# Expert weights of a mixture-of-experts layer loaded in two halves of the model dimension

## Chip, cores and metric

The kernel runs on one core of one Trainium2 chip. The metric is device time in microseconds (us) of one launch; lower is better. The time of the kernel before is the median of 3 runs.

## What is computed

One trunk layer (DEPTH = 1) over 384 tokens of width 1024 in f32: a parallel token mixer, then a fine-grained mixture of experts, then a norm. The part around the change is the mixture of experts:

```
h = rmsnorm(x) * (1 + scale) + shift
scores = sigmoid(h @ w_router)                  # 64 experts in 8 groups
combine = top-8 of the best 4 groups, normalised, x 2.5
hid = silu(h @ we_g[e]) * (h @ we_u[e])          # for each expert e: 1024 -> 256
routed = sum over e of (hid * combine[:, e]) @ we_d[e]      # 256 -> 1024
shared = (silu(h @ ws_g) * (h @ ws_u)) @ ws_d
out = routed + shared
```

The weights of one expert are gate 1024x256, up 1024x256 and down 256x1024, 1 MiB (1.049 MB) each in f32; all 64 experts have to come in from HBM once. With 384 tokens and 8 choices each, an expert has 48 tokens on average.

## The kernel before

The mixer comes first, then the router, then the experts. Experts are worked two at a time, as 32 pairs (`PAIRS`), p = 0 to 31. A pair gives each expert 64 slots (`SLOTS`) for its tokens; experts that have more tokens are finished afterwards by three "duo" rounds (`DUOS`), p = 32 to 34, which take 32 slots a time, with the weights loaded again for those experts (`load_item`), and by a loop over what is left.

For a pair p TensorE does: `gate_up(p)` (L1029, 16 matmuls that fill one bank: the loop runs over 8 chunks k of the model dimension and over the 2 experts n), `tokens_of(p + 1)` (L976, L979, the transposes of the next pair's gathered tokens), `slots_of(p + 2)` (L931), `hidden_T(p)` (L1041), `scatter(p - 1)` (L1063, the outputs of the pair before added to the tokens' rows), and `down(p)` (L1056, 8 matmuls). An f32 matmul stands as two in the trace, so gate_up shows 32 and down 16. VectorE and ScalarE turn the results of each step into the next one's input. GpSimd gathers the token rows of a pair with an indirect DMA (L520): 128 rows of 1088 f32 values, 4352 bytes; slots without a token are dropped by the bounds check.

The weights lie in `ring`, four places of one expert each. Pair p has slot s = p % 2, that is places 2s and 2s + 1, so a pair's weights overwrite those of pair p - 2. All weight loads are issued by SyncE (SP) on one DMA queue, in program order; each DMA is spread over the 16 DMA engines. Weights of pair p are loaded when its slot is free: gate and up after `gate_up(p - 2)` has counted the semaphore `gate_up_done`, and down after `down(p - 2)` has counted `down_done`. In the load of gate and up (L411, L412) each of the 128 partitions gets one contiguous piece of 8192 bytes: `w_eg` and `w_eu` are viewed so that partition i holds rows 8i to 8i + 7 of the matrix one after the other, and chunk k of the matmul takes row 8i + k of each partition. TensorE waits for all four loads of its pair by `gate_up_slot{s}`, 16 counts for each DMA:

```
sp.wait_ge(sem("gate_up_done"), p - 1)
for n in range(2):
    load_gate_up(sp, (2 * p + n) * P, 2 * s + n, f"gate_up_slot{s}")
sp.wait_ge(sem("down_done"), 2 * (p - 1))
for n in range(2):
    load_down(sp, (2 * p + n) * P, 2 * s + n, f"down_slot{s}")
```

Pairs 0 and 1 are loaded by `first_expert`, earlier, as soon as the mixer's weights have left the ring. Pairs 2 to 31 are loaded by the loop above.

Of the kernel before, what the change touches and what calls it, by code (L numbers as in the profile page):

```python
# [12 lines left out]
P = 128  # L13
D = 1024
KC = D // P
# [13 lines left out]
PAIRS = E // 2  # L29
# [11 lines left out]
CELL = 2048  # L41
# [3 lines left out]
EXPERT = 3 * CELL  # L45
# [135 lines left out]
def trunk_kernel(nc, A, outs, consts, dists):  # L181
    y_prompt, y_sample, new_f, new_b = outs
    ctx = ExitStack()
    with ctx:
        def sb(name, shape, dt=F32):
            return ctx.enter_context(nc.sbuf_tensor(name, shape, dt))

        ring = sb("ring", [P, NSLOT * EXPERT])
# [30 lines left out]
        def sem(name):  # L219
            if name not in sems:  # L220
                sems[name] = ctx.enter_context(nc.semaphore(name))
            return sems[name]
# [137 lines left out]
        w_eg = A["w_exp_gate"].rearrange("o e (p k) f -> (o e p) (k f)", p=P)  # L360
        w_eu = A["w_exp_up"].rearrange("o e (p k) f -> (o e p) (k f)", p=P)
# [45 lines left out]
        def load_gate_up(sp, row, e, landed):  # L407

            w = ring[:, e * EXPERT:(e + 1) * EXPERT]
            src = (lambda a: a[row:row + P, :]) if isinstance(row, int) else (lambda a: a[bass.ds(row, P), :])  # L410
            sp.dma_start(w[:, 0:CELL], src(w_eg)).then_inc(sem(landed), 16)  # L411
            sp.dma_start(w[:, CELL:2 * CELL], src(w_eu)).then_inc(sem(landed), 16)  # L412

        def load_down(sp, row, e, landed):

            w = ring[:, e * EXPERT:(e + 1) * EXPERT]
            src = w_ed[row:row + P, :] if isinstance(row, int) else w_ed[bass.ds(row, P), :]
            sp.dma_start(w[:, 2 * CELL:3 * CELL], src).then_inc(sem(landed), 16)
# [7 lines left out]
        def _(sp):  # L426
# [5 lines left out]
            for name in PIECES:  # L432
# [5 lines left out]
                landed = sem(f"piece_slot{PLACE[name]}")  # L438
# [36 lines left out]
            def load_item(n, e_slot, load, landed, count):  # L475
                there = sp.value_load(column(tab_valid, n), min_val=0, max_val=1)
                with sp.If(there > 0):
                    e = sp.value_load(column(tab_expert, n), min_val=0, max_val=E - 1)
                    load(sp, e * P, e_slot, landed)
                with sp.Else():  # L480
                    sp.sem_inc(sem(landed), count)

            for p in range(2, LAST + 1):
                s = p % 2
                if p == PAIRS:
                    sp.wait_ge(sem("table_ready"), 1)
                sp.wait_ge(sem("gate_up_done"), p - 1)
                for n in range(2):
                    if p < PAIRS:
                        load_gate_up(sp, (2 * p + n) * P, 2 * s + n, f"gate_up_slot{s}")  # L490
                    else:
                        load_item(2 * (p - PAIRS) + n, 2 * s + n, load_gate_up, f"gate_up_slot{s}", 32)
                sp.wait_ge(sem("down_done"), 2 * (p - 1))
                for n in range(2):
                    if p < PAIRS:
                        load_down(sp, (2 * p + n) * P, 2 * s + n, f"down_slot{s}")
                    else:
                        load_item(2 * (p - PAIRS) + n, 2 * s + n, load_down, f"down_slot{s}", 16)
# [109 lines left out]
        def _(pe):  # L608
# [70 lines left out]
            for k in range(KC):  # L679
                pe.wait_ge(sem("scaled_A" if k % 2 else "scaled_V"), k // 2 + 1)  # L680
                ins = mm(o[:, :], hT_scaled[:, k, 0:P], win0.rearrange("p (k n) -> p k n", k=KC)[:, k, :], start=(k == 0), stop=(k == KC - 1))
# [8 lines left out]
            for k in range(KC):  # L690
                q = k % 4 * 32
                ins = mm(o[q:q + 32, :], shift_rep[:, k, :], win0.rearrange("p (k n) -> p k n", k=KC)[:, k, :], start=(k < 4), stop=(k >= KC - 4))
# [7 lines left out]
            for g in range(4):  # L700
                ins = nc.tensor.transpose(o[:, g * P:(g + 1) * P], shift_row[:, g * P:(g + 1) * P], ident)
# [37 lines left out]
            for t in range(TT):  # L739
                for name, nat in (("q", q_nat), ("k", k_nat)):  # L740
# [5 lines left out]
                    for h in range(H):  # L746
                        ins = nc.tensor.transpose(o[:, h * P:(h + 1) * P], nat[:, t, h * P:(h + 1) * P], ident)
# [3 lines left out]
            for d in range(2):  # L751
                pe.wait_ge(sem("kw_ready"), d + 1)
                o = bank(f"state{d}")
                for h in range(H):
                    ins = mm(o[:, h * P:(h + 1) * P], kw[:, d, h * P:(h + 1) * P], v_nat[:, 0, h * P:(h + 1) * P], start=True, stop=True)
# [5 lines left out]
            for h in range(H):  # L761
                ins = mm(o[:, h * P:(h + 1) * P], kT[:, h, 0:P], qT[:, h, 0:P], start=True, stop=True)
            done(ins)
            for h in range(H):
                o = bank(f"sc_lat{h}")
                for j in range(2):
                    ins = mm(o[:, j * LAT:(j + 1) * LAT], kT[:, h, (1 + j) * P:(2 + j) * P], qT[:, h, CTX:T], start=True, stop=True)
# [4 lines left out]
            for h in range(H):  # L772
                ins = mm(o[:, h * P:(h + 1) * P], sc_sb[:, 4, h * P:(h + 1) * P], v_nat[:, 0, h * P:(h + 1) * P], start=True, stop=True)
            done(ins)
            pe.wait_ge(sem("state_in"), 32)
            for t in (1, 2):
                o = bank(f"o{t}")
                for h in range(H):
                    emptied(pe, f"sc_lat{h}")
                    for j in range(2):  # L780
                        ins = mm(o[:, h * P:(h + 1) * P], sc_sb[:, h, j * LAT + (t - 1) * P:j * LAT + t * P],
                                 v_nat[:, 1 + j, h * P:(h + 1) * P], start=(j == 0), stop=(j == 1))
                done(ins)
                for d, name in ((0, "cross_f"), (1, "cross_b")):
                    o = bank(f"{name}{t}")
                    for h in range(H):
                        ins = mm(o[:, h * P:(h + 1) * P], qT[:, h, t * P:(t + 1) * P], S0[:, d, h, :], start=True, stop=True)
# [17 lines left out]
            for m in range(KC):  # L805
# [6 lines left out]
                if m == 5:  # L812
                    for t in range(TT):
                        pe.wait_ge(sem("ret_ready"), t + 1)
                        o = bank(f"retT{t}")
                        for h in range(H):
                            ins = nc.tensor.transpose(o[:, h * P:(h + 1) * P], g_nat[:, t, h * P:(h + 1) * P], ident)
# [122 lines left out]
            for t in range(TT):  # L940
                for u in range(t + 1):
                    ins = mm(o[:, t * E:(t + 1) * E], cbf[:, 0 if u == t else 1, :], sel_bf[:, u, :], start=(u == 0), stop=(u == t))
            done(ins)
            o = bank("count")
            for t in range(TT):
                ins = mm(o[0:E, 0:1], sel_bf[:, t, :], cbf[:, 1, 0:1], start=(t == 0), stop=(t == TT - 1))
# [5 lines left out]
            for t in range(TT):  # L952
                ins = nc.tensor.transpose(o[0:E, t * P:(t + 1) * P], r_rank[:, t, :], ident)
# [44 lines left out]
            landed = LAST // 2 + 1  # L998
# [20 lines left out]
            def gate_up(p):  # L1019
                s = p % 2  # L1020
                if p:
                    pe.wait_ge(sem("xT_ready"), 2 * p)
                    pe.wait_ge(sem("hid_ready"), p)
                else:
                    last_in(0)
                pe.wait_ge(sem(f"gate_up_slot{s}"), 64 * (p // 2 + 1))
                for k in range(KC):
                    for n in range(2):
                        ins = mm(ps[0][n * SLOTS:(n + 1) * SLOTS, :], xT[:, k, n * SLOTS:(n + 1) * SLOTS], expert(2 * s + n)[0][:, k, :, :],  # L1029
                                 start=(k == 0), stop=(k == KC - 1))  # L1030
                ins.then_inc(sem("gate_up_done"), 1)

            def hidden_T(p):
# [104 lines left out]
            for p in range(LAST):  # L1138
                if p < PAIRS:
                    gate_up(p)  # L1140
                else:
                    pe.wait_ge(sem("xT_ready"), 2 * p)
                    pe.wait_ge(sem("hid_ready"), p)
                    pe.wait_ge(sem(f"gate_up_slot{p % 2}"), 64 * (p // 2 + 1))
                    gate_up_duo(p % 2)
                tokens_of(p + 1)
                if p + 2 < PAIRS:
                    slots_of(p + 2)
                elif p + 2 <= LAST:
                    slots_of_duo(p + 2)  # L1150
                hidden_T(p)
                if p:
                    scatter(p - 1)
                if p < PAIRS:
                    down(p)
                else:
                    pe.wait_ge(sem("hidT_ready"), p + 1)
                    pe.wait_ge(sem(f"down_slot{p % 2}"), 32 * (p // 2 + 1))
                    pe.wait_ge(sem("rest_ready"), 2 * p)
                    down_duo(p % 2)  # L1160
            scatter(LAST - 1)

            def further(q):
                p = q + LAST
                pe.wait_ge(sem("gate_up_slot1"), q * 64 + 64 * landed)
                pe.wait_ge(sem("xT_ready"), p * 2)
                pe.wait_ge(sem("hid_ready"), p)
                stand_alone(pe, "pe_passed")
                gate_up_duo(1)
                slots_next(q)  # L1170
                hidden_T(p)
                pe.wait_ge(sem("hidT_ready"), p + 1)
                pe.wait_ge(sem("rest_ready"), p * 2)
                pe.wait_ge(sem("down_slot1"), q * 32 + 32 * landed)
                stand_alone(pe, "pe_passed")
                down_duo(1)
                pe.wait_ge(sem("lo_ready"), p * 2 + 2)
                pe.wait_ge(sem("summed"), p * 6)
                stand_alone(pe, "pe_passed")
                for g in range(6):  # L1180
                    if g == 2:
                        pe.wait_ge(sem("expert_ready"), q + (DUOS + 2))
                    if g >= 4:
                        pe.wait_ge(sem("summed"), p * 6 + (g - 3))
                    scatter_duo_tile((slotT[:, 0, :], slotT_half[:, DUOS, :]), g)
                tokens_next(q)
# [872 lines left out]
```

## Time and profile before

| what | value |
|---|---|
| runs | 1014.66, 1017.45, 1017.86 us; median 1017.45 |
| the profiled execution | 1013.35 us, span 1011.4 us |
| granted TensorE clock, mean | 0.992 of full speed |
| busy: PE, DVE, ACT, POOL | 95%, 52%, 22%, 5% of the span |
| DMA traffic | 301.57 MB, mean 298 GB/s over the span |
| pairs 0 to 31 on TensorE | about 435 us to 950 us of the span |

The page shows one profiled execution, in us from the start of its span. Its own time is 1.95 us longer than its span, and 4.1 us below the median of the runs. PE is TensorE's matmuls, PEld its weight loads, DVE is VectorE, ACT is ScalarE, POOL is GpSimd, SP is SyncE; a "q" behind a name is the engine's queue of issues. The DMA share is the time that packets took, summed and divided by 16 engines; packets in flight on one engine overlap a little, so a full stretch reads slightly over 1. In the rows on DMA queues q1 holds what SyncE issues (the weights) and q0 what GpSimd issues (the gathers); packets of 4 bytes are the counts on a semaphore at the end of a DMA.

### The profile page before, as it was taken

Reading aid. Unit: us, or ns where it says so; the run is one execution under the profiler, and the core shown is the slowest. Engines: PE = TensorE matmul, PEld = TensorE weight load, DVE = VectorE, ACT = ScalarE, POOL = GpSimd, SP = SyncE. Lnnn points to the kernel's source line nnn. Section 1 sums busy time; section 2 is a strip of 40 time slices with the busy share of each in tenths; the row PEclk is TensorE's granted clock in tenths of the full one; section 3 lists DMA queues with packets and bytes.
Section 4 is the critical chain, followed back from the end, with each engine's and each line's share of the span. In section 5 each row is a group of like instructions: output and inputs, shape, how many; then the busy total and the mean of one; then the engine's idle time right before and its main releaser. Section 6 shows DMA issues by size and latency. Waiting matters only on the chain. (4 is left out here: it accounts for less than half of the span.)

```text
span 1011.4 us, 11592 instructions
## 1 busy us (share of the span) xinstructions
PE 961.5 (95%) x4287; PEld 449.4 (44%) x4322; DVE 524.6 (52%) x1089; ACT 221.2 (22%) x423; POOL 55.0 (5%) x71
## 2 busy tenths in 40 slices
PE   4999999999999999899999999999999999999891
PEld 2346445755655547634334343433434343343440
DVE  2202510885695944635454554545455454545666
ACT  4202102010000034222222222222222222222222
POOL 1010000100000000010000000000000000000000
PEclk9999999999999999999999999999999999999997
DMA  9992223207465469059999999999999999999921
GB/s 334 391 336 85 84 83 119 80 2 286 171 226 179 156 249 396 35 230 420 421 421 418 420 420 418 421 419 417 416 421 416 418 406 420 414 417 410 374 112 64
DMA packets 66587, 301.57 MB, mean 298 GB/s; under 512 B 6992, under 2 KB 7176, under 8 KB 39392
## 3 DMA queue, kind: packets, MB, share of 16 engines
q1 hardware_dynamic: 59376, 281.19, 69.5%
q0 software_dynamic: 7152, 19.60, 5.1%
q8 instruction: 36, 0.59, 0.2%
q14 instruction: 23, 0.19, 0.1%
HBM read 303.54 MB, written 3.80 MB: 304 GB/s over the span
## 5 line engine op out<-in xcount | busy, mean ns | idle before, releaser
L1029 PE MATMUL bank<-ring,QK 128*64 128x512 f32 x1024 | 225.2, 592 | 0.0
L1029 PEld LDWEIGHTS bank<-ring,QK 128*64 128x64 f32 x1024 | 73.5, 137 | 146.4 <-issue 146.4
L1912 DVE TENSOR_TENSOR hT<-bank,hT 128x512 f32<-128x512 f32 x210 | 129.2, 683 | 3.4 <-PE bank L1107 2.3
L1063 PE MATMUL bank<-Fm,VG 128*128 128x512 bf16 x544 | 123.2, 379 | 5.3 <-DVE S L1943 3.3
L1056 PE MATMUL bank<-ring,VG 128*64 128x512 f32 x512 | 116.9, 598 | 0.5 <-ACT VG L1388 0.5
L666 PE MATMUL bank<-ring,hT 128*128 128x512 f32 x240 | 103.8, 593 | 0.0
L1903 DVE SCALAR_TENSOR_TENSOR VG<-VG,cw,bank 128x256 f32<-128x256 f32 x32 | 15.4, 480 | 143.3 <-issue 136.9
L1921 DVE TENSOR_TENSOR Fm<-bank,Fm 128x512 f32<-128x512 f32 x64 | 44.3, 692 | 85.1 <-ACT Fm L1395 82.9
L673 PE MATMUL bank<-hT,ring 128*128 128x384 f32 x256 | 85.4, 487 | 0.0
L1063 PEld LDWEIGHTS bank<-Fm,VG 128*128 128x128 bf16 x576 | 56.3, 98 | 65.1 <-DVE S L1943 4.8
L1395 ACT CAST Fm<-bank 128x512 bf16<-128x512 f32 x64 | 37.5, 586 | 208.2 <-PE bank L1056 208.2
L666 PEld LDWEIGHTS bank<-ring,hT 128*128 128x128 f32 x240 | 45.4, 190 | 56.9 <-issue 56.3
L1056 PEld LDWEIGHTS bank<-ring,VG 128*64 128x64 f32 x512 | 33.9, 136 | 68.6 <-issue 68.0
L673 PEld LDWEIGHTS bank<-hT,ring 128*128 128x128 f32 x256 | 48.3, 190 | 34.5 <-issue 1.7
L1377 ACT ACTIVATE VG<-bank 128x256 f32<-128x256 f32 x35 | 13.4, 384 | 167.4 <-PE bank L1029 163.1
L1927 DVE TENSOR_TENSOR Fm<-Fm 128x512 bf16<-128x512 f32 x64 | 43.9, 686 | 2.8
L673 PE MATMUL bank<-Fm,ring 128*128 128x384 f32 x128 | 42.6, 486 | 0.0
L845 PE MATMUL bank<-ring,U 128*128 128x512 f32 x96 | 42.1, 594 | 0.0
L1398 ACT CAST Fm<-Fm 128x512 bf16<-128x512 f32 x64 | 39.7, 620 | 7.7 <-DVE Fm L1921 7.7
L1382 ACT COPY QK<-bank 128x512 f32<-128x512 f32 x70 | 37.6, 589 | 7.9 <-PE bank L976 7.9
L1297 ACT ACTIVATE S<-bank 128x384 f32<-128x384 f32 x16 | 7.8, 491 | 124.5 <-PE bank L673 124.5
L1459 DVE SCALAR_TENSOR_TENSOR AB<-ring,condr,AB 128x512 f32<-128x512 f32 x42 | 31.6, 752 | 1.5
(356 smaller groups left out, 889.6 us busy)
## 6 DMA issues: line engine op xcount, KB each, us to landing
ring<-in_w_exp_gate SPq DMA_DIRECT2D x69, 1024.0 KB
ring<-in_w_exp_up SPq DMA_DIRECT2D x69, 1024.0 KB
ring<-in_w_exp_down SPq DMA_DIRECT2D x69, 1024.0 KB
ring<-in_w_ada SPq DMA_DIRECT2D x12, 2048.0 KB, 10.3
ring<-in_w_in SPq DMA_DIRECT2D x10, 2048.0 KB, 16.9
ring<-in_w_four_out SPq DMA_DIRECT2D x2, 2048.0 KB, 8.1
ring<-in_w_out SPq DMA_DIRECT2D x2, 2048.0 KB, 11.1
ring<-in_w_ret_out SPq DMA_DIRECT2D x1, 2048.0 KB, 14.1
```

The source lines that it names most:

```text
L666: ins = mm(o[:, :], h[:, k, t * P:(t + 1) * P], w[:, k, :], start=(k == 0), stop=(k == KC - 1))
L673: ins = mm(o[:, 0:T], w[:, k, m * P:(m + 1) * P], rhs[:, k, :], start=(k == 0), stop=(k == kc - 1))
L845: ins = mm(o[:, :], mergedT[:, k, t * P:(t + 1) * P], w[:, k, :], start=(k == 0), stop=(k == KC - 1))
L1029: ins = mm(ps[0][n * SLOTS:(n + 1) * SLOTS, :], xT[:, k, n * SLOTS:(n + 1) * SLOTS], expert(2 * s + n)[0][:, k, :, :], start=(k == 0), sto ...
L1056: ins = mm(ps[2 + h][n * SLOTS:(n + 1) * SLOTS, :], hidT[:, j, n * SLOTS:(n + 1) * SLOTS], expert(2 * s + n)[1][:, j, h * 512:(h + 1) * 51 ...
L1063: ins = mm(ps[banks[g]][:, :], slotT[:, k, t * P:(t + 1) * P], y[:, h * 512:(h + 1) * 512], start=(n == 0), stop=(n == 2))
L1382: nc.scalar.copy(halves[n], ps[4 + n][:, :].rearrange("p (k s) -> p k s", k=4)).then_inc(sem("xT_ready"), 1)
L1395: nc.scalar.copy(y_hi[:, h * 512:(h + 1) * 512], ps[2 + h][:, :]).then_inc(sem("hi_ready"), 1)
L1398: nc.scalar.copy(y_mid[:, h * 512:(h + 1) * 512], y_rest[:, h * 512:(h + 1) * 512]).then_inc(sem("mid_ready"), 1)
L1912: v.tensor_tensor(into, o, into, ALU.add).then_inc(sem("summed"), 1)
L1921: v.tensor_tensor(y_rest[:, cut], ps[2 + h][:, :], y_hi[:, cut], ALU.subtract).then_inc(sem("rest_ready"), 1)
L1927: v.tensor_tensor(y_lo[:, cut], y_rest[:, cut], y_mid[:, cut], ALU.subtract).then_inc(sem("lo_ready"), 1)
```

## The change

The gate and up loads of pairs 2 to 31 are each cut in two along the model dimension. A half is 4 of the 8 rows that a partition holds: 4096 of its 8192 bytes. TensorE counts a new semaphore, `gate_up_half_done`, behind the matmuls of chunk k = 3, the last that reads the first half; SyncE then issues the four first halves (gate and up of two experts) of pair p when `gate_up(p - 2)` is half through, and the four second halves when it is through. TensorE still waits for both halves before `gate_up(p)`: the count it waits for is 128 a pair where it was 64. Loads of pairs 0 and 1, of the duo rounds, and all down loads are as they were.

```diff
+        def load_gate_up_half(sp, row, e, half, landed):
+
+            cut = slice(half * CELL // 2, (half + 1) * CELL // 2)
+            w = ring[:, e * EXPERT:(e + 1) * EXPERT]
+            sp.dma_start(w[:, 0:CELL][:, cut], w_eg[row:row + P, cut]).then_inc(sem(landed), 16)
+            sp.dma_start(w[:, CELL:2 * CELL][:, cut], w_eu[row:row + P, cut]).then_inc(sem(landed), 16)
+
...
                 if p == PAIRS:
                     sp.wait_ge(sem("table_ready"), 1)
+                if p < PAIRS:
+                    sp.wait_ge(sem("gate_up_half_done"), p - 1)
+                    for n in range(2):
+                        load_gate_up_half(sp, (2 * p + n) * P, 2 * s + n, 0, f"gate_up_slot{s}")
                 sp.wait_ge(sem("gate_up_done"), p - 1)
                 for n in range(2):
                     if p < PAIRS:
-                        load_gate_up(sp, (2 * p + n) * P, 2 * s + n, f"gate_up_slot{s}")
+                        load_gate_up_half(sp, (2 * p + n) * P, 2 * s + n, 1, f"gate_up_slot{s}")
...
-                pe.wait_ge(sem(f"gate_up_slot{s}"), 64 * (p // 2 + 1))
+                pe.wait_ge(sem(f"gate_up_slot{s}"), 64 + 128 * (p // 2))
                 for k in range(KC):
                     for n in range(2):
                         ins = mm(ps[0][n * SLOTS:(n + 1) * SLOTS, :], xT[:, k, n * SLOTS:(n + 1) * SLOTS], expert(2 * s + n)[0][:, k, :, :],
                                  start=(k == 0), stop=(k == KC - 1))
+                    if k == KC // 2 - 1:
+                        ins.then_inc(sem("gate_up_half_done"), 1)
                 ins.then_inc(sem("gate_up_done"), 1)
```

The counts that the duo rounds and the last loop wait for are raised to match.

On SyncE's queue, the place where the loads of pair 2 begin (`ring` is the weights' buffer, the names behind `in_` are the inputs), before the change:

```order
L411 DMA ring<-in_w_exp_gate 128x2048 [waits gate_up_done]
L412 DMA ring<-in_w_exp_up 128x2048
L411 DMA ring<-in_w_exp_gate 128x2048
L412 DMA ring<-in_w_exp_up 128x2048
L418 DMA ring<-in_w_exp_down 128x2048 [waits down_done]
L418 DMA ring<-in_w_exp_down 128x2048
```

Each later pair up to 31 repeats these six. The same place with the change:

```order
L418 DMA ring<-in_w_exp_gate 128x1024 [waits gate_up_half_done]
L419 DMA ring<-in_w_exp_up 128x1024
L418 DMA ring<-in_w_exp_gate 128x1024
L419 DMA ring<-in_w_exp_up 128x1024
L418 DMA ring<-in_w_exp_gate 128x1024 [waits gate_up_done]
L419 DMA ring<-in_w_exp_up 128x1024
L418 DMA ring<-in_w_exp_gate 128x1024
L419 DMA ring<-in_w_exp_up 128x1024
L425 DMA ring<-in_w_exp_down 128x2048 [waits down_done]
L425 DMA ring<-in_w_exp_down 128x2048
```

Ten DMAs stand where six stood, and the first four of them wait for TensorE's middle mark; no load has moved past a load of another matrix or pair. On TensorE no instruction moves.

## Rows read from the trace of the kernel before

**Rows 1.** The page: span, engine busy in 40 slices, DMA share and rate.

```profile
PE 961.5 (95%) x4287; PEld 449.4 (44%) x4322; DVE 524.6 (52%) x1089; ACT 221.2 (22%) x423; POOL 55.0 (5%) x71
...
PE   4999999999999999899999999999999999999891
...
DMA  9992223207465469059999999999999999999921
```

**Rows 2.** TensorE's timeline: start, length (us), line, output and inputs, count.

```profile
465.01 7.04 PE L1029 MATMUL bank<-ring,QK 128*64 128x512 f32 x32
...
481.09 7.04 PE L1029 MATMUL bank<-ring,QK 128*64 128x512 f32 x32
...
706.11 7.04 PE L1029 MATMUL bank<-ring,QK 128*64 128x512 f32 x32
713.08 0.66 PE L976 MATMUL bank<-consts_sb,VG 128*128 128x128 f32 x4
...
898.99 7.04 PE L1029 MATMUL bank<-ring,QK 128*64 128x512 f32 x32
...
932.73 7.04 PE L1029 MATMUL bank<-ring,QK 128*64 128x512 f32 x32
...
963.04 3.64 PE L1093 MATMUL bank<-ring,QK 128*32 128x256 f32 x64
```

**Rows 3.** Who TensorE waited for, 400 us to 1011 us: total, times, longest.

```profile
PE bank L1063 <- DVE S L1943: 3.3, 3, 1.1
...
PE bank L976 <- DMA VG<-h_rows,idx: 1.2, 1, 1.2
```

**Rows 4.** SyncE's issues, from the timeline: start, length, line, what.

```profile
442.05 0.33 SPq L411 DMA_DIRECT2D ring<-in_w_exp_gate  x1
...
706.32 0.80 SPq L418 DMA_DIRECT2D ring<-in_w_exp_down  x2
713.19 0.33 SPq L411 DMA_DIRECT2D ring<-in_w_exp_gate  x1
```

**Rows 5.** Windows: length, busy time by engine, clock, DMA share, GB/s.

```profile
405.00:442.00 37.00, 34.13 (x147) 19.61 (x147) 18.50 (x74) 5.98 (x12) 4.07 (x5) 0.95 0.14 49
...
480.00:560.00 80.00, 79.74 (x385) 31.44 (x388) 41.89 (x85) 20.33 (x41) 4.96 (x5) 1.00 1.01 420
...
800.00:880.00 80.00, 79.74 (x387) 31.50 (x390) 41.52 (x86) 20.69 (x40) 4.96 (x5) 1.00 1.01 414
```

**Rows 6.** DMA queues, 480 us to 920 us: packets, MB, share of 16 engines.

```profile
q1 hardware_dynamic: 23579, 171.70, 94.1%
q0 software_dynamic: 4029, 11.80, 6.7%
```

**Rows 7.** DMA queues, 1002 to 1011 us, outputs in pieces of 4096 bytes.

```profile
q1 hardware_dynamic: 432, 1.57, 42.6%
```

**Rows 8.** DMA queues, 100 to 200 us, mixer weights in pieces of 2048 bytes.

```profile
q1 hardware_dynamic: 4160, 8.39, 24.0%
```

**Rows 9.** TensorE's weight loads in the middle of down, around its count.

```profile
703.97 0.14 PEld L1056 LDWEIGHTS bank<-ring,VG 128*64 128x64 f32 x2 [0.29 <-issue]
704.40 0.14 PEld L1056 LDWEIGHTS bank<-ring,VG 128*64 128x64 f32 x2 [0.29 <-issue]
704.83 0.14 PEld L1056 LDWEIGHTS bank<-ring,VG 128*64 128x64 f32 x2 [0.28 <-issue]
```

**Rows 10.** Gathers, DMA issues of 480 to 920 us: count, us to landing.

```profile
QK<-h_rows,idx POOLq DMA_INDIRECT x14, 9.0
...
VG<-h_rows,idx POOLq DMA_INDIRECT x13, 9.0
```

More of the change, by code:

```diff
@@ L1143, in _ @@
                     pe.wait_ge(sem("hid_ready"), p)
-                    pe.wait_ge(sem(f"gate_up_slot{p % 2}"), 64 * (p // 2 + 1))
+                    pe.wait_ge(sem(f"gate_up_slot{p % 2}"), 64 * (p // 2 + 1) + 64 * (PAIRS // 2 - 1))
                     gate_up_duo(p % 2)
@@ L1164, in further @@
                 p = q + LAST
-                pe.wait_ge(sem("gate_up_slot1"), q * 64 + 64 * landed)
+                pe.wait_ge(sem("gate_up_slot1"), q * 64 + (64 * landed + 64 * (PAIRS // 2 - 1)))
                 pe.wait_ge(sem("xT_ready"), p * 2)
```

## Prediction

> **What bounds the kernel now.** I read the page first: TensorE is busy 95% of the span, and the DMA line stands at 9 through the whole expert part [rows 1]. Two resources look full, so the question is which one waits for the other. TensorE's timeline answers it: gate_up of pair 2 starts at 465.01, of pair 3 at 481.09, of pair 29 at 898.99, which is 27 periods of 16.07 us with no drift [rows 2]. In its waits no weight load appears: one gather cost 1.2 us, and the longest of the rest is VectorE near the end [rows 3]. So TensorE sets the pace of the pairs, and a load that is earlier by itself gains nothing there. Now the DMA side. Before 442 the engines are nearly idle (share 0.14); from 480 on the share is 1.01 at 414 to 420 GB/s [rows 5]. A share that stays full means that the loads are always behind the place where they could start; the transfers are as close to being the bound as TensorE is. What counts is how much room lies between the landing of a pair's weights and their use, and how fast it shrinks.
>
> **The room before.** Pair 2's loads are issued at 442.05 [rows 4] and, about 1 us later, the queue begins to move. A pair needs 6 loads of 1.049 MB, 6.29 MB; the weights queue moved 171.70 MB in 440 us [rows 6], 0.390 MB/us. Gate and up of pair 2 are 4.19 MB: 10.8 us, so 453.8, and TensorE uses them at 465.01, 11.2 us later. For pair 29 it is 27 x 6.29 + 4.19 = 174.1 MB: 446 us, so 889.1, against 898.99: 9.9 us of room. Pair 33 (a duo round that loads two whole experts again) needs 199.2 MB, so 953.5, against 963.04 [rows 2]: 9.5 us. These are means over 16 engines, and TensorE waits for the last engine. No view shows the engines one by one. My bound for the last: a gather has 128 rows but on average 96 with a token; if an engine serves 8 neighbouring rows, some carry 8 and some none, 2 rows above the mean of 6, at 174 ns (below), 0.35 us a pair and 9.7 us by pair 29. That end leaves 0.2 us of room, and since TensorE did not wait, there is no less. I take the middle, a lag of 4.9 at pair 29 and 5.2 at pair 33: room 5.0 and 4.3 us.
>
> **Part 1, the earlier issue: a head start of 3.5 us, once.** gate_up takes 6.97 us from 706.11 to the next step at 713.08 [rows 2], its middle is 3.5 us before the end. SyncE issued at 713.19, 0.1 us after the end [rows 4], and will issue the first half 3.5 us earlier. For pair 2 that finds idle engines, so the whole stream of transfers begins 3.5 us earlier, at 439.5. For the later pairs the queue is full anyway: an earlier place in it moves nothing. Down loads are issued at their old times.
>
> **Part 2, smaller packets: about 0.33 us more transfer a pair.** Per pair 512 packets of 8192 bytes become 1024 of 4096, the bytes are the same. What is a packet's own cost? In 480 to 920 the weights took 94.1% of 16 x 440 us, 6625 us for 20,959 packets of 8192 (171.70 MB; the others are 4-byte counts): 316 ns. The gathers took 6.7%, 472 us for 2,711 rows of 4352 (11.80 MB): 174 ns [rows 6]. A line through both has 13 ns that don't depend on size. But the gathers hold more counts, 1,318 for 2,711 rows against 2,620 for 20,959; if a count costs as much as a packet's fixed part, that part is 7 ns. I take 10 ns, between them: 512 x 10 / 16 engines is 0.32 us, with 0.01 for the 64 counts of four more DMAs: 0.33 us a pair. Lower end: the output stores in pieces of 4096, 61.3 us for 384 packets, 160 ns [rows 7], so 2 x 160 - 316 = 4 ns, 0.13 us a pair. Upper end: mixer loads in pieces of 2048, 384 us for 4,096, 94 ns [rows 8]; 4 x 94 - 316 = 60 ns for 3 more packets, 20 ns, 0.64 us a pair. The gathers are the nearest rows (loads in the same stretch), hence 10.
>
> The Trainium skill, "DMA: Bandwidth & Descriptors", section "Why small descriptors are slow (HBM only)", gives a packet a fixed overhead of some 3 cycles; at the 850 MHz that the page has for the fabric this is 3.5 ns, an estimate of 0.11 us a pair, and with it the sum would be no change. The rows of the loads are two to four times dearer, and I go by them.
>
> **Part 3, what costs nothing.** TensorE's new count: the weight loads on both sides of down's middle count stand 0.43 us apart like all others [rows 9], so 0, at most 10 ns x 32. SyncE: four more issues of about 0.4 us, while its issues at 706.32 (0.80 us) and 713.19 [rows 4] leave 6 us free; nobody waits for it, and a blocked SyncE has a full queue behind it. Its new wait for the middle mark stands in front of the second halves only, whose mark comes later anyway. Gathers take 9.0 us [rows 10] on a queue that shares the engines; the first one's 1.2 us wait [rows 3] may move by up to 1 us either way, I put 0.
>
> **The sum.** At pair 29 (28 split pairs) transfers are later by 28 x 0.33 - 3.5 = 5.7 us against 5.0 of room: TensorE waits 0.7. At pair 33 (30 split pairs) by 9.9 - 3.5 = 6.4 against 4.3: 2.1 in all (the first wait is part of it, since the waits are measured against the same old times). About 2 us: the profiled 1013.35 would be 1015.4. It lies 4.1 us below the median, for which no row gives a reason; I put the same 2 us on the median of 1017.45: **1019.5 us**, within 0.3% (3.05 us, about what a measurement of this kernel can tell from no change).
>
> **Rivals.**
> - **The transfers become the bound well before the end: slower.** The place is the wait of gate_up for `gate_up_slot` from pair 25 or so on. It decides when 30 x price - 3.5 exceeds the room by over 3.05. With the room at its lower end it is 6.4 - 0.2 = 6.2: 1023.7; with the 20 ns end 19.1 - 3.5 - 4.3 = 11.3: 1028.8. If the 4 us of the timed runs above the profiled one are already waits for weights, the added transfers count in full, 6.4: 1023.9. For it: share 1.01, room that fell from 11.2 to 9.9 already, a wait for the last of 16 engines. Against: TensorE shows no such wait in this trace. 0.36.
> - **No wait: the same.** At 4 to 7 ns a packet the added transfer is 3.9 to 6.6 us, less 3.5: 0.4 to 3.1, inside the room of 4.3. Or the room is the mean engine's 9.5. The change then does nothing to the end, 1017.5: TensorE waited for no weights and still waits for none. 0.26.
> - **A gain.** The timed runs wait for weights, and the packets cost nothing: -3.5, 1014.0. Against it: every row of smaller packets has a price above zero, and at 0.12 us a pair the head start is spent. 0.07.
> - **Each DMA's fixed time enters the queue: much slower.** If the queue stood for 2 us at each DMA, 4 more would add 8 us a pair and 240 us in all, near 1250. Six DMAs a pair already fit in 16.07 us with the packets alone filling 1.01, so there is no such gap [rows 5]. 0.01. The Trainium skill, "DMA: Bandwidth & Descriptors", section "Bandwidth", says to batch DMAs to at least 1 MiB, and its fit has about 2.0 us fixed for each; these halves are 0.5 MiB. The trace disagrees as long as the queue is full.
>
> **How the numbers follow.** The forecast (a late wait of 0.3 to 3 us) has 0.30, no wait 0.26: same 0.56. Slower by over 0.3% 0.36 + 0.01, faster 0.07. The range leaves out 2 in 10: below, the runs of before reach to 1014.66 and a gain to 1014.0, so 1014.5; above it takes in the lower room and the bound runs (1023.7, 1023.9) and half the way to the 20 ns end: 1026.
>
> **What would show it.** The page after should have the DMA share still full, about 15,400 more packets, and the rate of the stretches of [rows 5] lower by up to 2%. The queue rows should give about 163 ns for a 4096-byte packet. SyncE's first issue for pair 2 should stand near 438.5, and that of later pairs 3.5 us after gate_up starts. TensorE's period must stay 16.07 until pair 28; then the gaps of gate_up grow, 0.7 us at pair 29, about 2 in all by pair 33. A period above 16.07 before pair 25 would mean that the transfers bind and the first rival holds; no longer gap anywhere, that the room or the price was misjudged; a shorter time, that weights were waited for in a way the trace of before does not show.

## The result, and the profile after

The change makes the kernel slower. 14 executions of each were timed: 1018.94 us with the change (1017.27 to 1021.06), 1013.61 us before (1010.92 to 1017.86); the ratio is 1.0049, with a 95% interval of 1.0036 to 1.0062, which is 5.0 us (3.6 to 6.3). The forecast of 1019.5 us lies close to 1018.94, but that is partly luck. It stood on a median of 1017.45 from three runs and 2 us of loss; the loss is 5 us and the median of more runs of before is 1013.6.

The page of the kernel with the change: engines with their busy time, and 40 slices of the span.

```profile
span 1016.8 us, 11712 instructions
...
PE 962.6 (95%) x4287; PEld 452.0 (44%) x4322; DVE 524.4 (52%) x1089; ACT 221.1 (22%) x423; POOL 54.9 (5%) x71
...
DMA  9992223108465368179999999999999999999931
...
DMA packets 83868, 301.58 MB, mean 297 GB/s; under 512 B 8912, under 2 KB 9096, under 8 KB 72032
```

TensorE has the same 4287 matmuls and a busy time longer by 1.1 us in a span longer by 5.4 us [rows 1]. The DMA line is as full as before, for the same bytes. The packets are 83,868 for 66,587, that is 17,281 more: 15,360 of them come from the cuts (30 pairs of 512) and 1,920 are counts of the added DMAs, which the 15,400 of the prediction left out.

Who TensorE waited for, 400 us to 1011 us, with the change:

```profile
PE bank L1040 <- DMA ring<-in_w_exp_up: 4.3, 5, 1.8
PE bank L1076 <- DVE S L1956: 3.3, 3, 1.2
...
PE bank L1106 <- DMA ring<-in_w_exp_up: 0.5, 1, 0.5
```

The first and the last line are new against [rows 3]: gate_up (L1040, L1106 in a duo round) waits for weights. The wait of 1.2 us for the first gather is gone. TensorE's timeline shows where the waits are:

```profile
463.90 7.04 PE L1040 MATMUL bank<-ring,QK 128*64 128x512 f32 x32
...
801.67 7.09 PE L1040 MATMUL bank<-ring,QK 128*64 128x512 f32 x32
...
819.74 7.09 PE L1040 MATMUL bank<-ring,QK 128*64 128x512 f32 x32 [1.78 <-DMA ring<-in_w_exp_up]
...
901.65 7.09 PE L1040 MATMUL bank<-ring,QK 128*64 128x512 f32 x32 [0.29 <-DMA ring<-in_w_exp_up]
...
919.77 7.09 PE L1040 MATMUL bank<-ring,QK 128*64 128x512 f32 x32 [1.83 <-DMA ring<-in_w_exp_up]
...
968.43 3.66 PE L1106 MATMUL bank<-ring,QK 128*32 128x256 f32 x64 [0.45 <-DMA ring<-in_w_exp_up]
```

Pair 2 starts at 463.90, 1.1 us earlier than before (465.01 in [rows 2]), since the gather came in time. (That gather came in time too in a run below that loads pair 2 as before, so this gain isn't shown to be the change's doing.) With the old period of 16.07 pair 23 would start at 801.4 and does at 801.67. From pair 24 on (819.74, 2.3 us behind the old rhythm) TensorE is no longer what sets the pace. Pair 29 starts at 901.65, 3.8 us behind it, and pair 33 at 968.43 where it was 963.04: 5.39 us later, exactly the difference of the spans.

DMA queues from 480 to 920 us, with the totals of that stretch ahead:

```profile
DMA packets 42704, 181.07 MB, mean 412 GB/s; under 512 B 5604, under 2 KB 5604, under 8 KB 35803
...
q1 hardware_dynamic: 38726, 169.17, 95.3%
q0 software_dynamic: 3950, 11.53, 6.6%
```

The packet time of a half is in these rows. Of the 35,803 packets under 8 KB 5,604 are counts and 2,649 are gathered rows (11.53 MB of 4352 bytes), so 27,550 are halves. They carry 112.8 MB; the other 56.3 MB are 6,876 whole packets. 95.3% of 7040 us is 6709 us; less 6,876 x 316 ns it leaves 4536 us for the halves, 165 ns each with their counts. Two of them take 13 ns more than one of 316 [rows 6]. This is time summed over packets that overlap: the DMA share of a whole stretch rose too, from 1.01 [rows 5] to 1.02, here with the change:

```profile
480.00:560.00 80.00, 79.74 (x387) 31.51 (x390) 41.74 (x85) 20.68 (x40) 4.95 (x5) 1.00 1.02 414
```

What reaches TensorE is less, and can be read directly. The traces hold every count on a semaphore, so also the last count of a pair's gate and up loads, which is when the pair may start:

| pair | before: landed, used | room | with the change: landed, used | room |
|---|---|---|---|---|
| 2 | 456.80, 465.01 | 8.2 | 456.22, 463.90 | 7.7 |
| 3 | 473.00, 481.09 | 8.1 | 472.71, 479.98 | 7.3 |
| 12 | 618.90, 625.75 | 6.9 | 620.91, 624.64 | 3.7 |
| 20 | 747.53, 754.33 | 6.8 | 752.04, 753.22 | 1.2 |
| 21 | 764.05, 770.41 | 6.4 | 769.17, 769.31 | 0.1 |
| 29 | 893.97, 898.99 | 5.0 | 901.51, 901.65 | 0.1 |
| 33 | 957.89, 963.04 | 5.2 | 968.29, 968.43 | 0.1 |

A room of 0.14 us is a wait: TensorE starts that long after the last count, in every pair that waits. Already before the change the room shrinks, from 8.1 to 5.0 us, because the landings come every 16.15 us (pairs 3 to 20) and TensorE's steps every 16.07. With it the landings go from 0.3 us early at pair 3 to 4.5 late at pair 20, 0.28 us a pair, and since TensorE starts 1.1 us earlier as well, the room is used up at pair 21. Pair 2, whose first loads were issued 3.3 us earlier, landed only 0.6 us earlier.

And the start of the stream, in windows: with the change first, then before.

```profile
443.00:449.00 6.00, 5.54 (x28) 2.06 (x28) 2.53 (x7) 2.75 (x6) 1.04 (x1) 1.00 1.02 322
449.00:452.00 3.00, 3.00 (x16) 1.01 (x14) 1.85 (x5) 0.77 (x2) 0.00 (x0) 1.00 1.02 412
```

```profile
443.00:449.00 6.00, 5.54 (x29) 2.04 (x30) 2.53 (x7) 2.76 (x6) 1.04 (x1) 1.00 0.96 378
449.00:452.00 3.00, 3.00 (x18) 1.00 (x16) 1.71 (x5) 0.63 (x2) 0.00 (x0) 1.00 1.02 428
```

The engines are full with the change (share 1.02) and move only 322 GB/s; from 449 on it is 412. That is a loss which the prediction did not have. The window before, 378 GB/s, contains the start of the first packets at 443 and is otherwise whole.

SyncE, finally, spent far more time on its issues: the load of one gate matrix, 480 to 920 us (count, then ns of one as least, median and most), first before and then with the change.

```profile
L411 SPq DMA_DIRECT2D ring<-in_w_exp_gate x54: 327/377/441, 488.2 to 906.9; - x54
```

```profile
L418 SPq DMA_DIRECT2D ring<-in_w_exp_gate x108: 327/1062/6695, 483.6 to 912.5; - x108
```

### The profile page after: what moved, and what is told of

Same layout as the page of the kernel before. It is cut to its first block and busy times, and to the rows that moved or that the text cites. A ratio compares the mean times of both kernels' runs of the same rounds, so it can differ in the third digit from the quotient of the medians.

```text
span 1016.8 us, 11712 instructions
## 1 busy us (share of the span) xinstructions
PE 962.6 (95%) x4287; PEld 452.0 (44%) x4322; DVE 524.4 (52%) x1089; ACT 221.1 (22%) x423; POOL 54.9 (5%) x71
## 2 busy tenths in 40 slices
DMA packets 83868, 301.58 MB, mean 297 GB/s; under 512 B 8912, under 2 KB 9096, under 8 KB 72032
## 5 line engine op out<-in xcount | busy, mean ns | idle before, releaser
L1040 PE MATMUL bank<-ring,QK 128*64 128x512 f32 x1024 | 225.6, 593 | 4.3 <-DMA ring<-in_w_exp_up 4.3
L1040 PEld LDWEIGHTS bank<-ring,QK 128*64 128x64 f32 x1024 | 76.3, 137 | 149.3 <-issue 149.3
L677 PEld LDWEIGHTS bank<-ring,hT 128*128 128x128 f32 x240 | 45.4, 190 | 56.9 <-issue 56.3
```

The source lines that it names most:

```text
L677: ins = mm(o[:, :], h[:, k, t * P:(t + 1) * P], w[:, k, :], start=(k == 0), stop=(k == KC - 1))
```

## Experiments

Each run was timed against the kernel before on the same chip. The medians and ratios are of those executions. Before itself had 1014.7 to 1015.0 us on these chips.

**Halves, none early.** Both halves are issued after `gate_up_done`.

```diff
-                if p < PAIRS:
-                    sp.wait_ge(sem("gate_up_half_done"), p - 1)
-                    for n in range(2):
-                        load_gate_up_half(..., 0, ...)
                 sp.wait_ge(sem("gate_up_done"), p - 1)
+                if p < PAIRS:
+                    for n in range(2):
+                        load_gate_up_half(..., 0, ...)
...
-                    if k == KC // 2 - 1:
-                        ins.then_inc(sem("gate_up_half_done"), 1)
```

> Halves as in the change, but both are issued after gate_up_done, so nothing is issued early. Theory A (the split costs 0.32 us of transfer a pair, the room at the end is 4 to 5 us, and the early issue gave almost nothing because the first packets ran slow): the same as the change, 1.005 of before, within 1.5 us. Theory B (the early issue gave its 3.5 us and the split costs more, about 0.43 us a pair): 3.5 us worse than the change, 1.0085. Theory C (the early issue itself disturbs, by its place in the queue or by the new count on TensorE): back at 1.000.

1023.11 us, ratio 1.0097 (1.0079 to 1.0115): 9.8 us, twice the change's loss. So the early issue helps, by 4 to 5 us in the medians and by 2.5 to 3.1 in the landings at pair 3 (table in the next section), the split alone costs more than the change does, and theory C (the early issue or TensorE's new count does the harm) falls: both are gone here and the loss is larger. Theory A's claim that the head start was worth nothing falls too. But its slow first packets are there, moved with the issue: here the stream begins at about 443, and the slow place reaches to 452.

```profile
443.00:449.00 6.00, 5.54 (x31) 2.15 (x30) 2.53 (x7) 2.71 (x6) 1.04 (x1) 1.00 0.92 302
449.00:452.00 3.00, 3.00 (x18) 1.00 (x16) 2.13 (x5) 1.04 (x2) 0.00 (x0) 1.00 0.91 277
```

**Only pair 2 split.** A function `is_split(p)` picks the pairs that are split and early; the counts that TensorE waits for follow from it.

```diff
+        def is_split(p):
+            return p == 2
...
-                if p < PAIRS:
+                if is_split(p):
                     sp.wait_ge(sem("gate_up_half_done"), p - 1)
...
                     if is_split(p):
                         load_gate_up_half(..., 1, ...)
+                    elif p < PAIRS:
+                        load_gate_up(sp, (2 * p + n) * P, 2 * s + n, f"gate_up_slot{s}")
```

> Only pair 2 is split and issued early; all later pairs are loaded whole. Theory A and B: no wait for weights anywhere, 1.000, or 0.999 if the first gather lands in time as it did in the change (1.1 us). Theory A adds: the packets of 4096 bytes in the first 9 us of the stream are slow again (some 200 ns, 330 GB/s between 440 and 449 us). Theory C: a loss that goes with the early issue would be one thirtieth, 1.000 too, so this run tells only A's slow start from B's full head start: with B the rate from 443 us on is above 400 GB/s.

1013.38 us, 0.9996 (0.9982 to 1.0010): no loss. In its profile TensorE waits for no DMA at all, the first gather included, and pair 2 starts at 463.96. The slow start is there: 304 GB/s from 443 to 449 at a share of 1.01, and 406 after it, and pair 2 lands only 0.6 us earlier than before, at 456.16. So that cost comes with the first split pair, and the early issue of one pair is as harmless as the head start is useless where nothing waits.

**TensorE starts on the first halves.** The second halves have their own semaphore.

```diff
+                    if k == KC // 2 and p > 1:
+                        pe.wait_ge(sem(f"gate_up_late{s}"), 64 * (p // 2))
```

> The change, but TensorE starts gate_up when the first halves have landed and waits for the second halves in front of chunk k = 4, on a semaphore of their own. Theories A and B: the same transfers are needed 3.5 us later, so of the 5.3 us about 2 stay: 1.002, and a wait for a DMA shows in the middle of gate_up. Theory C: unchanged, 1.005.

> TensorE starts on the first halves, a second time: its profiled execution took 1016.1 us, as the theory of late transfers has it (2 to 3 us above before), its other executions 1021 to 1025 at a mean granted clock of 0.984 to 0.989. If the clock falls because TensorE now waits in many short pieces, the runs are again spread over 1016 to 1025, the clock again below 0.990 in the slow ones, and the ratio is 1.005 to 1.009. If that was chance: 1.002 to 1.003.

The profiled execution of the first set took 1016.12 us, the other five 1021 to 1025, and the set has 1.0085 (1.0069 to 1.0100), so I ran it a second time beside the change. The second set has 12 executions from 1013.74 to 1024.17, median 1019.40, ratio 1.0037 (1.0014 to 1.0060), where the change itself has 1.0054 (1.0034 to 1.0074). The intervals of the two sets don't overlap. The first excludes the 3 us that were expected to come back; the second holds both 1.002 and the change's own 1.0054. The profile of the first set shows where TensorE waits now:

```profile
886.14 3.65 PE L1042 MATMUL bank<-ring,QK 128*64 128x512 f32 x16 [0.25 <-DMA ring<-in_w_exp_up]
...
965.85 3.66 PE L1108 MATMUL bank<-ring,QK 128*32 128x256 f32 x64 [1.95 <-DMA ring<-in_w_exp_up]
```

gate_up is now cut in its middle, with short waits of 0.2 us for the second halves at pairs 28 to 30. The long wait has moved to pair 33 (L1108), a duo round whose weights are whole loads: it needs all of them at its start, and the queue in front of them is as late as ever. The profile of the second set is of a late execution (1022.88 us), and it answers why they spread. Its waits for weights are the same, 2.5 us for 2.6. But its span is 6.8 us longer: 3.7 us are there before pair 0 starts (438.80 for 435.12), and 3.0 behind pair 33. In both parts the granted clock is lower than in the first execution: 0.96 for 1.00 from 20 to 60 us, 0.91 for 0.95 from 405 to 442, and 0.62 for 0.94 from 994 to 1003, while the last matmuls run. From 60 to 405 us and from 442 to 994 it is 1.00 in both. So the difference between these two executions is the clock's, and the waits that are left, 2.5 us for 4.8 and 3.1 in the two traces of the change, suggest that starting on the halves gives a little back; the medians can't show it.

**The change again,** on the chip of the second set:

> The change itself, beside the others on one chip, since halves issued late took 1.0097 where the change had 1.0049. If the early issue is worth its 3.5 us: 1.005 again. If the two chips differ and it is worth nothing: 1.009.

1019.62 us, 1.0054 (1.0034 to 1.0074). The change has the same loss on two chips, and its interval lies below that of the run with none early.

**Quarters.** Four parts of 2048 bytes, at marks after k = 1, 3, 5 and the end (the edit against the change; SyncE's loop over the four parts and the counts are left out).

```diff
-            cut = slice(half * CELL // 2, (half + 1) * CELL // 2)
+            cut = slice(half * CELL // 4, (half + 1) * CELL // 4)
...
-                    if k == KC // 2 - 1:
-                        ins.then_inc(sem("gate_up_half_done"), 1)
+                    if k in (1, 3, 5):
+                        ins.then_inc(sem("gate_up_quarter_done"), 1)
```

> Quarters in place of halves: packets of 2048 bytes, 16 gate and up DMAs a pair in place of 8, each quarter issued at its mark. Theory A: three cuts a packet in place of one, 3 x 0.32 and some for the counts, 1.0 to 1.1 us a pair, 30 to 33 us, less the room of 4 to 5: 1.026. If the price falls with smaller pieces: 1.015. Theory C (what costs is the count or the issue, not the packets): 1.01 or less.

1042.24 us, 1.0282 (1.0258 to 1.0306): 28.6 us. The earliest quarter is issued 5.2 us before the end of gate_up instead of 3.5, and it does not help: the landings get later by 0.98 us a pair from pair 3 to pair 15, for three cuts a packet, where one cut took 0.29. That the price grows with the number of pieces is the main thing here. Its waits, 400 us to 1060 us, and one of SyncE's issues from the timeline:

```profile
PE bank L1042 <- DMA ring<-in_w_exp_up: 20.5, 15, 3.4
```

```profile
714.61 5.12 SPq L418 DMA_DIRECT2D ring<-in_w_exp_gate  x1
```

An issue that took 0.4 us before the change took 5.12: SyncE itself is held, so early marks were partly lost. The halves have this as well (median 1.06 us, up to 6.7, above). It comes with the smaller packets (even and odd partitions, with as many DMAs as the change, have at most 0.7 us for a gate or up load), and not with the loss: the last 15 pairs split (below) have issues of up to 5.7 us and no loss, the extra transfer (next) has a median of 0.33 us for a gate load and loses.

**Whole loads and an extra transfer.** The kernel before, with one more small DMA a pair.

```diff
+EXTRA = 204
+        spare = sb("spare", [P, 2, EXTRA])
...
                         load_gate_up(sp, (2 * p + n) * P, 2 * s + n, f"gate_up_slot{s}")
+                        if n:
+                            if p > 3:
+                                sp.wait_ge(sem(f"spare_in{s}"), 16 * (p // 2 - 1))
+                            sp.dma_start(spare[:, s, :], w_ed[(2 * p) * P:(2 * p + 1) * P, 0:EXTRA]).then_inc(sem(f"spare_in{s}"), 16)
```

> The kernel before with whole loads (8192-byte packets, old issue times, no new count on TensorE) and one more DMA a pair of 128 x 816 bytes into a spare tile, 8 packets of some 39 ns and a count on each engine: 0.32 us a pair, the price put on the split. If added transfer time alone makes the loss (theory A): 30 x 0.32 = 9.6 less the room of 4 to 5: 1.005. If it takes the smaller packets or the early issue themselves: 1.000.

1022.92 us, 1.0064 (1.0040 to 1.0089): 6.5 us. The landings get later by 0.31 us a pair, with no small weight packet, nothing early and TensorE's program untouched, and that makes a loss like the change's. Its waits have the same form:

```profile
PE bank L1035 <- DMA ring<-in_w_exp_up: 3.8, 9, 1.7
```

**Twice the DMAs, packets whole.** Two tries at the price of a DMA by itself. In the first each gate and up load is cut into partitions 0 to 63 and 64 to 127, in the second into even and odd partitions.

```diff
+            for h in range(2):
+                at = slice(h * 64, (h + 1) * 64)
+                sp.dma_start(w[at, 0:CELL], w_eg[row + h * 64:row + (h + 1) * 64, :]).then_inc(sem(landed), 16)
+                sp.dma_start(w[at, CELL:2 * CELL], w_eu[row + h * 64:row + (h + 1) * 64, :]).then_inc(sem(landed), 16)
```

```diff
-                at = slice(h * 64, (h + 1) * 64)
+                at = slice(h, P, 2)
...
-                sp.dma_start(w[at, 0:CELL], w_eg[row + h * 64:row + (h + 1) * 64, :]).then_inc(sem(landed), 16)
+                sp.dma_start(w[at, 0:CELL], w_eg[row + h:row + P:2, :]).then_inc(sem(landed), 16)
```

> The kernel before with each gate and up load of pairs 2 to 31 cut by partitions, two DMAs of 64 partitions with packets of 8192 bytes: as many DMAs as the change has, none smaller in its packets, none early. If the packets make the price: four counts more a pair, 0.04 us on each engine, 1.2 us in all, inside the room: 1.000. If a DMA has a fixed time of its own in the queue: 1.005 or more.

> The price of a DMA by itself, mended: each gate and up load of pairs 2 to 31 in two DMAs, of the even and of the odd partitions, packets of 8192 bytes. In the run with partitions 0 to 63 and 64 to 127 apart the packets took 577 ns in place of 315, so it could not tell. If that came from 64 neighbouring partitions as a target: packets are back at 315 ns here, and four more counts a pair fit in the room, 1.000 to 1.001. If it came from DMAs of 64 rows as such: again 1.4. If a DMA has a fixed time in the queue: packets at 315 ns, but a rate below 414 GB/s and 1.005 or more.

The first took 1427.70 us in its fastest execution and 1492.24 in its slowest (median of six 1465.01), the second 1014.62 us, 0.9995 (0.9980 to 1.0009). Their weights queues from 480 to 920 us, first the neighbouring and then the even and odd partitions:

```profile
q1 hardware_dynamic: 14007, 94.95, 95.5%
```

```profile
q1 hardware_dynamic: 25393, 172.10, 94.3%
```

The second has 172.10 MB in 21,008 packets of 8192 bytes: 6639 us, 316 ns each, as before, with four more DMAs a pair. Its landings don't get later from pair to pair (0.00 us a pair from 3 to 15). So a DMA and its counts cost nothing that the time shows, and the packet size is what remains. Only at the start of its stream are these DMAs slow too, with whole packets:

```profile
449.00:452.00 3.00, 3.00 (x18) 1.00 (x16) 1.65 (x3) 1.63 (x4) 0.20 (x1) 1.00 1.00 360
```

The first had 94.95 MB in 11,591 packets, 6723 us: 580 ns each, and is a case of its own (last section).

**Which pairs are split.** With `is_split` as above, all but pair 2, and the last 15 alone.

```diff
-            return p == 2
+            return 2 < p < PAIRS
```

```diff
-            return p == 2
+            return 17 <= p < PAIRS
```

> The change without its first pair: pair 2 is loaded whole at the old time, pairs 3 to 31 in halves, early. No idle queue is met, so there is no head start, and no slow first packets. If the two cancel in the change (3.3 us gained, 2 to 3 us lost in the first 9 us of the stream): 29 x 0.32 = 9.3 less the room of 4 to 5, 1.005, the same as the change within 1 us. If the head start counts in full: 3 us worse than the change, 1.008.

> Only pairs 17 to 31 are split. 15 x 0.32 = 4.8 us of transfer, as much as the room of 4 to 5 us: 1.000 to 1.001, with at most a short wait for weights near pair 33. If the loss went in proportion to the split pairs, with no room: half of the change's, 1.0025.

All but pair 2: 1023.50 us, 1.0084 (1.0057 to 1.0111), 8.5 us. Without the head start it is 3.5 us worse than the change, though one pair less is split; the intervals leave some 3 us either way. In the landings at pair 3 the difference is 1.6 to 2.2 us. The slow place is here as well, now at pair 3, the first with halves: 354 GB/s at a full share.

```profile
460.00:466.00 6.00, 6.00 (x30) 2.13 (x30) 3.29 (x7) 1.34 (x3) 0.62 (x1) 1.00 1.00 354
```

The last 15: 1016.03 us, 1.0001 (0.9988 to 1.0014). Half of the split pairs do not cost half of the loss, they cost nothing to speak of. In its profile TensorE waits 1.2 us in all for weights, at the very end, at 886 and 919 us. There is a room, and the loss begins where it is used up. Its first halves, issued at about 680 us, show no slow place:

```profile
678.00:684.00 6.00, 6.00 (x32) 2.05 (x27) 1.59 (x5) 0.97 (x2) 0.00 (x0) 1.00 1.01 419
684.00:690.00 6.00, 6.00 (x32) 2.83 (x32) 5.36 (x11) 1.48 (x4) 0.99 (x1) 1.00 1.02 415
```


## Why the prediction was right and wrong

**What bounds the kernel** was right: TensorE with no wait for weights before, DMA engines full beside it, and the room between them as the quantity that decides. The runs with 15 and 30 split pairs (0 and 5 us) show the threshold. The size of the room was right as well: 5.0 us at pair 29, as forecast, and 5.2 at pair 33 for 4.3. The lag of 4.9 us behind the mean engine, which came from a guess on dropped rows, fits the landing at 893.97 (889.1 for the mean engine) exactly; that there is already a lag of 3.0 us at pair 2 (456.80 for 453.8) doesn't fit a lag that grows from zero, so this is in part luck.

**Part 1**, the head start, is the term that was mis-sized. It was right at the issue (SyncE's first issue stands at 438.75 for 442.05, 3.3 us). What failed is the next step, "For pair 2 that finds idle engines, so the whole stream of transfers begins 3.5 us earlier": pair 2 landed 0.6 us earlier, and 1.2 in the second trace of the change. About 0.3 us of what is missing is the price of its own cuts; the rest went in the slow first 9 us, which the forecast did not have. That slow start does not come from the early issue: pair 3 lands late by 2.1 us with none early, 1.2 with pair 2 whole and 1.3 with even and odd partitions, of which the cuts' own price is 0.6 us at most. Beside the run with none early, the early issue is worth 2.5 to 3.1 us.

**Part 2**, the price of the smaller packets, was right: 0.33 us a pair was forecast, and the landings got later by 0.28 to 0.29 in both traces of the change, 0.34 with none early. With 0.98 for the three cuts of the quarters this is 9 to 11 ns a cut, for the 10 that I took between 7 and 13. The 13 ns of packet time in the rows after would be 0.42 us a pair, but part of it overlaps.

**Part 3**, what costs nothing, held for the time: TensorE's count is not in the loss (none early, no count: larger loss), and DMAs by number are free (1014.62 us). But SyncE's issues were put at 0.4 us each with 6 us free, and had a median of 1.06: from 760 to 920 us they fill 147 of 160 us, where they filled 26. As the forecast said, nobody waited for that, since the queue in front was full.

**The sum again.** In the table, times are against before, each trace set to its own start of pair 0. The columns are how late the landing of pair 3 was, how much later each further pair landed (mean of pairs 3 to 15), the sum of both at pair 33 less the room of 5.0, and how late TensorE started pair 33 in fact. (28 pairs behind pair 3 are split, in the last line 15.)

| trace | pair 3 | us a pair | sum | measured |
|---|---|---|---|---|
| the change | -0.4 | 0.29 | 2.7 | 5.3 |
| the change again | -1.0 | 0.29 | 2.1 | 2.9 |
| none early | 2.1 | 0.34 | 6.6 | 7.0 |
| all but pair 2 | 1.2 | 0.29 | 4.3 | 6.1 |
| extra transfer | 1.6 | 0.31 | 5.3 | 7.5 |
| quarters | 1.6 | 0.98 | 24.0 | 24.5 |
| last 15 (pairs 17 to 27) | 0.1 | 0.31 | 0 | 0.4 |

With only pair 2 split, and with even and odd partitions, the landings gain or lose nothing from pair to pair (0.00), and pair 33 starts 1.3 us earlier than before, the wait for the first gather. The sum finds the large and the small losses and falls short by 0.4 to 2.6 us, never too long. In the first trace of the change 2.9 us are added at pairs 30 to 33, in the second 0.6. That rest is in no term, and its cause stays open. The forecast for pair 29, 0.7 us, compares with 2.7 (901.65 for 898.99), and its 2.1 us at pair 33 with 5.3 and, in the second trace, 2.9.

The time of an execution also holds a part that isn't a wait for weights. In the second trace the time behind pair 33 is 1.7 us longer than before, 50.1 for 48.4, and the granted clock is 0.57 from 994 to 998 us, where TensorE works on its last matmuls after being busy for 1.2 of the 4 us before. All but pair 2 has 51.3 us there, none early, the extra transfer and the quarters 50.1; the first trace of the change has 48.4 and a clock of 1.00 up to 1004 us, and its last matmuls are done by then. The mean granted clock of the 12 executions of the change is 0.9892, of the 25 of before beside them 0.9905. Whether a later end brings the lower clock more often was not tested.

**The rivals.** What came is the first rival: transfers that are the bound before the end, with a loss over 0.3%, which had 0.36. Its place is right (pair 24, "from pair 25 or so on"), its three cases are not what came: a room of 0.2 us (5.2), a price of 20 ns (9 to 11), or waits for weights in the runs of before, for which nothing speaks. The forecast's own case (0.30) had the same wait with 2 us of it. The gain and the fixed time of each DMA fell, the second by the even and odd partitions: the advice of the Trainium skill ("DMA: Bandwidth & Descriptors", section "Bandwidth") to batch at least 1 MiB does not bind here, where the queue is never empty. The 3-cycle overhead of a packet in the Trainium skill ("DMA: Bandwidth & Descriptors", section "Why small descriptors are slow (HBM only)"), 3.5 ns by my estimate, is about a third of the 9 to 11 ns measured.

**The 4.1 us between the profiled execution and the median** had no row. The executions do have one: beside the change, the kernel before took 1010.59 us at a mean granted clock of 0.994, 1013.02 to 1013.72 at 0.992, and 1019.98 at 0.986. Over these 25 executions time and mean clock go together (the square of their correlation is 0.88), and the traces show the same: the last-15 kernel does nothing new before pair 15, and its profiled execution starts pair 0 at 438.77 for 434.93, with a granted clock of 0.96 for 1.00 from 20 to 60 us and 0.91 for 0.95 from 405 to 442. The clocks of the three runs shown at first are not on record; that they were on the slow side of this is likely but not shown. No trace of before has a wait for weights, which one rival supposed.

## What to carry to other kernels

When the DMA share is full for hundreds of microseconds and the consumer still never waits, work out the room from bytes and starts, and ask of each change how much transfer time it adds per step: here 0.3 us a step was invisible for 15 steps and cost 5 us by 30. The counts on the semaphores give the room directly, pair by pair. Issuing a load earlier into a full queue moves it only once, at the start of the stream; paying for that with packets of half the size costs at every step. If a load has to be cut, cut it so that each packet keeps its length, and look at which partitions each part reaches: even and odd cost nothing here, the two halves of the partitions cost over 400 us.

## What the runs showed that was not expected

- Loads into 64 neighbouring partitions: the packets of 8192 bytes took 580 ns in place of 316, and the queue moved 94.95 MB where it moved 172.10 MB with as many DMAs a pair to every second partition. No run here shows the mechanism. It cost over 400 us, with TensorE waiting 336.8 us for weights in the trace.
- The first DMAs of 0.5 MiB run slow where they come near the start of the stream: with the change 472 halves (532 packets less 60 counts, 102.0% of 16 x 6 us) took 207 ns each from 443 to 449 us, later ones 165 ns. Without the early issue the slow place reaches to 452, with pair 2 whole at 460 to 466, where the queue was full; even and odd partitions have it with whole packets. With pair 17 as the first split pair it is missing. The extra transfer doesn't have it (421 GB/s from 447 to 450 us), though its pair 3 is 1.6 us late as well. So it is neither the packet size nor an idle queue alone. It stays open.

```profile
q1 hardware_dynamic: 532, 1.93, 102.0%
```

- The executions of one kernel differ by where the granted clock falls for a short time, and a trace shows it. The late execution of the kernel that starts on the halves (1022.88 us) has the same waits for weights as the early one (1016.12) and is later by 3.7 us before the first pair and by 3.0 behind the last weights, with a lower clock in both places (0.62 for 0.94 from 994 to 1003 us). A median of a few executions can move by most of what this change cost: 1017.45 us from three runs of before, 1013.61 from 14.
